# One decoder step on one core: the mixing and the routing of a block of tiles set in steps between the expert operations of the block before

## The reference, cut to what matters

```
g     = gelu(y);  y_s5 = rmsnorm(g * sigmoid(g @ w_glu), s5_norm_w)           # w_glu 1024 x 1024
y_m2  = group_rmsnorm(y_m2 * silu(z)) * m2_norm_w                             # two groups of 512
x     = x + concat([y_s5, y_m2]) @ w_out                                      # w_out 2048 x 1024
h     = rmsnorm(x, norm_ffn_w);   q = (h @ w_q) as 8 heads x 2 halves x 128   # w_q 1024 x 2048
s     = q . sub_keys (128 keys for each of the 16 halves)
sv,si = top_k(s, 16);  cand = sv[0][:, None] + sv[1][None, :];  cv, cpos = top_k(cand, 16)
idx   = si[0][cpos // 16] * 128 + si[1][cpos % 16];   gate = softmax(cv)      # 8 x 16 = 128 experts a row
x     = x + sum over the 128 experts: gate * gelu(u_tab[idx] . h) * v_tab[idx]
y     = rmsnorm(x, final_norm_w)
```

## Time and profile before

| | us |
|---|---|
| median of 3 runs (lowest to highest) | 4684.44 (4682.33 to 4685.42) |
| time of the profiled execution | 4684.25 |
| its span | 4682.5 |
| `mix_out` and the first routing, 1352.4 to 1891.6 | 539.20 |
| expert operations, 1891.6 to 4682.5 | 2790.90 |

### The profile page before, as it was taken

The page is one execution under the profiler, slowest core; times in us unless marked ns, Lnnn a source line. Parts: engine busy times, 40 slices in busy tenths (PEclk is TensorE's granted clock), DMA queues, the critical chain, the costliest instruction groups (busy, mean ns, idle before and its releaser), DMA issues.

```text
span 4682.5 us, 54327 instructions
## 1 busy us (share of the span) xinstructions
PE 2876.1 (61%) x17688; PEld 1481.5 (32%) x17688; DVE 2462.9 (53%) x4924; ACT 1290.2 (28%) x3117; POOL 1411.9 (30%) x1547
## 2 busy tenths in 40 slices
PE   8999590745559995554654744645645546447444
PEld 5766460723334444221311411411312213114110
DVE  1000529248831113576576675674675765766754
ACT  1110020112222321333333333333333333333332
POOL 3000320301100000444444444444443444444443
PEclk9999755866779997665755755756757658658555
DMA  4111300121131112899999999999999999999998
GB/s 163 52 50 36 75 2 2 43 101 30 39 160 66 46 54 97 349 421 420 415 421 400 421 421 405 420 420 404 420 419 400 421 419 405 421 407 420 421 415 362
DMA packets 258478, 1271.27 MB, mean 271 GB/s; under 512 B 63984, under 2 KB 98672, under 8 KB 118128
## 3 DMA queue, kind: packets, MB, share of 16 engines
q0 software_dynamic: 156672, 1140.92, 58.8%
q1 hardware_dynamic: 101536, 127.12, 8.2%
HBM read 1225.69 MB, written 40.09 MB: 270 GB/s over the span
## 4 chain that ended last, share of the span: by engine, by line
DMA 40%; issue 7%; PE 6%; ACT 4%; DVE 4%; POOL 1%; POOLq 0%; SPq 0%; DVEq 0%; ACTq 0%
DMA pe_ring<-in_uv,pe_index_now 39%; PE pe_acc L1858 3%; DVE pe_ring L1781 2%; PE pe_ps_q L1831 2%; ACT pe_mark L1629 1%; ACT pe_weight L1631 1%; PE pe_ps_t L1851 1%; ACT L1629 1%; DVE pe_work_a L1662 1%; POOL pe_ring L1570 1%; ACT L1620 1%; DMA pe_w_q<-in_w_q 0%; DVE pe_pos L1714 0%; DVE pe_work_b L1715 0%; PE pe_ps_s L1841 0%
## 5 line engine op out<-in xcount | busy, mean ns | idle before, releaser
L1781 DVE CUSTOM_DVE_ANT_0 pe_ring<-pe_ring,pe_h_rep 128x1024 f32<-128x1024 f32 x1088 | 1330.7, 1226 | 961.3 <-DMA pe_ring<-in_uv,pe_index_now 881.3
L1858 PE MATMUL pe_acc<-pe_ring,pe_weight 128*32 128x256 f32 x8704 | 1018.5, 560 | 1232.3 <-ACT pe_weight L1631 1203.4
L1570 POOL DMA_INDIRECT pe_ring<-in_uv,pe_index_now x1088 | 1198.0, 1101 | 1471.2 <-PE pe_acc L1858 1275.3
L1858 PEld LDWEIGHTS pe_acc<-pe_ring,pe_weight 128*32 128x32 f32 x8704 | 210.8, 131 | 1973.1 <-ACT pe_weight L1631 1863.6
L1629 ACT ACTIVATE pe_mark<-pe_eye,pe_dot 128x32 f32<-128x32 f32 x1088 | 349.4, 321 | 1744.1 <-DVE pe_dot L1781 1690.3
L1631 ACT ACTIVATE pe_weight<-pe_mark,pe_gate_now 128x32 f32<-128x32 f32 x1088 | 349.5, 321 | 35.1
L1831 PE MATMUL pe_ps_q<-pe_h_t,pe_w_q 128*128 128x128 f32 x2304 | 329.5, 303 | 1.9 <-DMA pe_w_q<-in_w_q 1.9
L1831 PEld LDWEIGHTS pe_ps_q<-pe_h_t,pe_w_q 128*128 128x128 f32 x2304 | 302.7, 213 | 60.1 <-issue 57.8
L372 PE MATMUL pj_bank<-pj_w_in,pj_normed_t 128*128 128x512 f32 (+1 forms) x720 | 267.6, 529 | 5.7 <-DMA pj_w_in<-in_w_in 5.7
L1392 PE MATMUL mo_ps_out<-mo_w_out,mo_both_t 128*128 128x512 f32 x576 | 251.1, 594 | 14.8 <-DVE mo_both_t L1342 11.9
L378 PE MATMUL pj_bank<-pj_normed_t,pj_w_in 128*128 128x128 f32 x1728 | 195.2, 275 | 0.0
...
## 6 DMA issues: line engine op xcount, KB each, us to landing
pe_ring<-in_uv,pe_index_now POOLq DMA_INDIRECT x1088
...
```

The source lines that it names most:

```text
L1570: nc.gpsimd.indirect_dma_start(out=ring[:, p, :], out_offset=None, in_=D["uv"], in_offset=bass.IndirectOffsetOnAxis(ap=row, axis=0)).then_ ...
L1781: V.tensor_tensor_reduce(out=ring[:, p, 0:D_MODEL], in0=ring[:, p, 0:D_MODEL], in1=h_rep[:, g % 2, :], scale=1.0, scalar=0.0, op0=ALU.mult ...
L1858: last = T.matmul(acc[j * PER:(j + 1) * PER, g % 2, 0:COLS], lhs(j), src[:, j * COLS:(j + 1) * COLS], start=first, stop=final)
```

## The change

`mix_out` becomes empty. `route_and_experts` now does mixing and routing for blocks of tiles: tile 0 alone, then tiles 1 and 2, tiles 3 to 5, tiles 6 to 8. Block 0 is done in an opening, with no expert operation beside it. Block 1 is set between the 128 operations of tile 0, block 2 between the 256 of tiles 1 and 2, block 3 between the 384 of tiles 3 to 5; tiles 6 to 8 have nothing between theirs. `block_steps` lists the steps of a block with a due time each, and `after[n]` holds the steps that follow operation n on every engine. 42% of the operations of a window (less 26) take the mixing, the others queries and keys. All loops are unrolled.

No weight matrix is held any more. `w_glu`, `w_out` and `w_q` are cut into 20 pieces of 256 columns ([128, 8, 256], 1.05 MB, rows of 1 KB in DRAM), loaded by SP into the two buffers of `w_buf`, once for every block. The load of a piece waits until the piece two before has been used. The gate matmuls have the weights as the stationary side and the block's tokens (128, 256 or 384) as the moving one, and so have the queries; the gate's result comes out transposed, and its norm is summed by a matmul with ones. The output matmuls move 256 columns of the weights for one tile's half. Chunk c of the gate matmuls waits for the sigmoid of chunk c - 2.

The ring has 7 slots instead of 8. `x_mid` stays in SBUF for the block, is stored to DRAM and read back as `x_now` tile by tile. Index and gate of a tile are double-buffered, so POOL copies no index. The keys of a block go through four units of four halves each, 16 steps a unit, each step for all tiles of the block. The places of the steps, in operations from the start of the window:

| | tile 0 (block 1) | tiles 1, 2 (block 2) | tiles 3 to 5 (block 3) |
|---|---|---|---|
| gate matmuls | 9 to 19 | 27 to 44 | 42 to 70 |
| output matmuls | 25 to 36 | 54 to 83 | 85 to 130 |
| h and its transposes | 39, 40 | 88 to 93 | 138 to 146 |
| queries and scores | 42 to 83 | 96 to 188 | 150 to 294 |
| keys | 54 to 101 | 122 to 227 | 191 to 354 |

```diff
@@ -1242,179 +1242,12 @@
 
 
 def mix_out(nc, D):
-
 def mix_out(nc, D):
...
+    pass
...
@@ -1423,482 +1256,693 @@
 
     PAIR = 2 * PH
     LEAST = -3.0e38
-    RING = 8
-    OPS = SLOTS
+    RING = 7
+    WB = 2
     GROUPS, PER = 4, 32
     COLS = D_MODEL // GROUPS
-    USES = OPS // RING
-    HALF = OPS // 2
-    UNITS, UNIT = PAIR // 4, 4
-    ROUTE_STEPS = 64
-    EVERY = OPS // ROUTE_STEPS
-    ROUTE_LINKS = UNITS * 4 + 27
-
-    SQUARES, NORM, TURN, H_T, QUERY = 3, 5, 6, 7, 8
-    Q_COPY, SCORE, SCORE_COPY, KEYS = QUERY + UNIT + 1, QUERY + UNIT + 2, QUERY + UNIT + 4, QUERY + UNIT + 5
-    SUMS = KEYS + UNIT * UNITS
-    EXP = SUMS + 16
-    CHOICE = SUMS + 22
-    assert CHOICE + 1 < (OPS - RING) // EVERY - 2
-    REP, REP_COPY, NOW_COPY = 16, 20, 14
-    assert GROUPS * PER == P and RING < HALF
+    BLOCK_OF = ((0,), (1, 2), (3, 4, 5), (6, 7, 8))
+    NB = max(len(tiles) for tiles in BLOCK_OF)
+    FIRST = [tiles[0] for tiles in BLOCK_OF]
+    HOME = {k: b for b, tiles in enumerate(BLOCK_OF) for k in tiles}
+    NT = MAIN_TILES * SLOTS + SAMPLE
+    NG = NT // PER
+    UNITS, UNIT = 4, 4
+    PIECES = 4 + 8 + PH
+    GLU, OUT, QUERY = 0, 4, 12
+    def block_steps(nb):
+        ev = []
+        add = lambda t, name, *args: ev.append((t, name, args))
+        for i in range(nb):
+            t = 8 * i
+            add(t, "sp_y", i)
+            add(t, "sp_x0", i)
+            for dt, name in ((2, "act_g"), (3, "dve_gate"), (3, "pe_g"), (4, "act_gt"), (4, "act_sq"), (5, "dve_mn"), (6, "pe_m"), (7, "dve_mt")):
+                add(t + dt, name, i)
+        g0 = 8 * (nb - 1) + 6
+        done = {}
+        for c in range(KT):
+            for dt, name in ((0, "pe_glu"), (1, "act_sig"), (2, "dve_s5"), (3, "act_ss"), (4, "pe_ss")):
+                add(g0 + 2 * c + dt, name, c)
+            done[GLU + c // 2] = g0 + 2 * c
+        r0 = g0 + 2 * KT + 3
+        add(r0, "act_r")
+        add(r0 + 1, "dve_r")
+        for c in range(KT):
+            add(r0 + 2 + c // 2, "dve_n", c)
+        o0 = r0 + 6 - nb
+        for q in range(4):
+            for half in range(2):
+                for i in range(nb):
+                    add(o0 + (2 * q + half) * nb + i, "pe_o", q, half, i)
+                done[OUT + 2 * q + half] = o0 + (2 * q + half) * nb + nb - 1
+            for i in range(nb):
+                add(o0 + (2 * q + 2) * nb + i, "dve_o", q, i)
+        h0 = o0 + 8 * nb + 1
+        for i in range(nb):
+            for dt, name in ((0, "act_hs"), (0, "sp_xm"), (1, "dve_h"), (2, "pe_h"), (3, "act_ht")):
+                add(h0 + 2 * i + dt, name, i)
+        q0 = h0 + 2 * nb + 2
+        for j in range(PAIR):
+            for dt, name in ((0, "pe_q"), (1, "act_q"), (2, "pe_s"), (3, "act_s")):
+                add(q0 + 3 * j + dt, name, j)
+            done[QUERY + j // 2] = q0 + 3 * j
+        for u in range(UNITS):
+            k0 = q0 + 12 * u + 13
+            for n in range(16):
+                add(k0 + n, "dve_k", u, n)
+            add(k0 + 12, "act_e", u)
+        for s in range(PIECES):
+            add(0 if s < WB else done[s - WB], "sp_w", s)
+        ev.sort(key=lambda e: e[0])
+        return ev, q0, ev[-1][0] + 1
+    opening = []
+    after = [[] for n in range(NT)]
+    for b, tiles in enumerate(BLOCK_OF):
+        ev, q0, last = block_steps(len(tiles))
+        if b == 0:
+            opening += [(name, (b,) + args) for t, name, args in ev]
+            continue
+        s, room = FIRST[b - 1] * SLOTS, len(BLOCK_OF[b - 1]) * SLOTS - 26
+        split = int(0.42 * room)
+        for t, name, args in ev:
+            n = s + (t * split // q0 if t < q0 else split + (t - q0) * (room - split) // (last - q0))
+            after[n].append((name, (b,) + args))
+    for k in range(TILES):
+        n = k * SLOTS
+        for back, name in ((31, "sp_x"), (20, "dve_hn"), (23, "pe_c"), (22, "dve_c")):
+            (after[n - back] if k else opening).append((name, (k,)))
+    for G in range(NG):
+        for back, name in ((16, "pe_rep"), (15, "act_rep")):
+            (after[G * PER - back] if G else opening).append((name, (G,)))
+        for on, name in ((0, "act_sum"), (1, "pe_add"), (3, "act_root"), (5, "dve_fin"), (6, "sp_st")):
+            after[min(G * PER + PER + on, NT - 1)].append((name, (G,)))
+    uses = [(name, args) for steps in [opening] + after for name, args in steps if name in ("pe_g", "pe_m", "pe_h", "pe_c", "pe_rep")]
+    TURN = {use: n for n, use in enumerate(uses)}
...
+            def weights(b, s):
+                W = PIECES * b + s
+                if W >= WB:
+                    b0, s0 = divmod(W - WB, PIECES)
+                    if s0 < OUT:
+                        sp.wait_ge(glu_made, KT * b0 + 2 * s0 + 2)
+                    elif s0 < QUERY:
+                        sp.wait_ge(out_made, outs(b0, (s0 - OUT) // 2, s0 % 2, size(b0) - 1))
+                    else:
+                        sp.wait_ge(q_made, PAIR * b0 + 2 * (s0 - QUERY) + 2)
+                if s < OUT:
+                    rows = D["w_glu"][:, :, s * COLS:(s + 1) * COLS]
+                elif s < QUERY:
+                    q, half = divmod(s - OUT, 2)
+                    rows = D["w_out"][:, KT - KT * half:2 * KT - KT * half, q * COLS:(q + 1) * COLS]
+                else:
+                    rows = D["w_q"][:, :, (s - QUERY) * COLS:(s - QUERY + 1) * COLS]
+                sp.dma_start(w_buf[:, W % WB], rows).then_inc(w_in[W % WB], 16)
+            def step(name, args):
+                if name == "sp_w":
+                    weights(*args)
...
+                if name == "act_sig":
+                    b, c = args
+                    C = KT * b + c
+                    act.wait_ge(glu_made, C + 1)
+                    if C >= 2:
+                        act.wait_ge(s5_made, C - 1)
+                    A(sig[:, c % 2, 0:width(b)], bg[:, c % 2, 0:width(b)], ACT.Sigmoid).then_inc(sig_ready, 1)
...
+            def keys(b, u, n):
...
+                if n == 0:
+                    dve.wait_ge(s_ready, UNITS * (U + 1))
+                    settle(dve, settled)
+                    for j, i in each:
+                        last = V.max(out=best[:, j, i, 0:8], in_=score[:, j, i, :])
+                    chain.link(last)
+                    settle(dve, settled)
...
+                if name == "dve_c":
+                    k = args[0]
+                    u = TURN["pe_c", args]
+                    dve.wait_ge(turned, u + 1)
+                    V.transpose(choice[:, k % 2], ps_t[:, 0:2, :]).then_inc(taken, 1)
+                    dve.wait_ge(taken, u + 1)
+                    V.tensor_copy(index[:, k % 2, :], choice[:, k % 2, 0, :]).then_inc(index_ready, 1)
...
+                if name == "pe_glu":
+                    b, c = args
+                    W, C = PIECES * b + GLU + c // 2, KT * b + c
+                    if c == 0:
+                        pe.wait_ge(taken, TURN["pe_g", (b, size(b) - 1)] + 1)
+                    if c % 2 == 0:
+                        pe.wait_ge(w_in[W % WB], 16 * (W // WB + 1))
+                    if c >= 2:
+                        pe.wait_ge(sig_ready, C - 1)
+                    for kk in range(KT):
+                        last = T.matmul(bg[:, c % 2, 0:width(b)], w_buf[:, W % WB, kk, c % 2 * P:(c % 2 + 1) * P], wide(in_t_all, b)[:, kk, :],
+                                        start=kk == 0, stop=kk == KT - 1)
+                    last.then_inc(glu_made, 1)
...
+                if name == "pe_o":
+                    b, q, half, i = args
+                    W = PIECES * b + OUT + 2 * q + half
+                    if i == 0:
+                        pe.wait_ge(w_in[W % WB], 16 * (W // WB + 1))
+                    if (q, half, i) == (0, 0, 0):
+                        pe.wait_ge(taken, TURN["pe_m", (b, size(b) - 1)] + 1)
+                        pe.wait_ge(sig_ready, KT * b + KT)
+                    if half == 0 and q * size(b) + i == 2:
+                        pe.wait_ge(r_root, b + 1)
+                    if (q, half, i) == (0, 1, 0):
+                        pe.wait_ge(s5_ready, KT * b + KT)
+                    if q * size(b) + i >= 4 and half == 0:
+                        pe.wait_ge(out_taken, kept(b, q, i) - 4)
+                    src = wide(s5_t_all if half else m2_t_all, b)
+                    for kk in range(KT):
+                        last = T.matmul(bg[:, (q * size(b) + i) % 4, 0:COLS], src[:, kk, i * P:(i + 1) * P], w_buf[:, W % WB, kk, :],
+                                        start=half == 0 and kk == 0, stop=half == 1 and kk == KT - 1)
+                    last.then_inc(out_made, 1)
...
+            for n in range(NT):
+                k, G, p = n // SLOTS, n // PER, n % RING
+                if n % SLOTS == 0:
+                    pe.wait_ge(x_now_in, 16 * k + 16)
+                if n % PER == 0:
+                    if G >= 2:
+                        pe.wait_ge(y_ready, G - 1)
```

(5 more changed lines are left out.)

946 lines of the change are left out of this document (435 added, 511 removed).

## The result

The change is slower, by 0.4%: 4701.53 us (median of 6 runs, 4696.99 to 4707.38) against 4684.22 for the kernel before in the same session, ratio 1.0038 (95% interval 1.0025 to 1.0051). The forecast was 4655 and faster. 4701.53 lies inside the forecast's wide range, but on the other side of the kernel before. The profiled execution has a span of 4695.2, 42 more than the 4653 of the sum.

The account below looks back on a forecast made before the run. The prediction took the expert stage to be bound by DMA bytes. First gather at 1528, plus 2980 of bytes, plus 145 of stalls made a span of 4653 us, time 4655, range 4565 to 4772.

Parts of the forecast that it names:

- Stalls: 54 + 45 + 15 + 20 + 10, about 145: Expert stage: keys 54, gate 45, output 15, loads and chain of h 20, tile boundaries 10; 60 to 240 us.
- 364 saved: Start of the stage: first expert gather at about 1528 instead of 1891.6, 364 us saved.
- 18 us of keys: Tiles 1 and 2: three tiles' keys on DVE take 301 us against 283, 18 lost; tiles 3 to 5 none.
- the gate "near nothing": Gate phase after tile 0: PE and ACT overlap, 6.6 us of PE against 6.5 of DMA, near nothing lost at full clock.
- the output "covered": Output phase after tile 0: matmuls covered at full clock; the 15 us term came from tile 0's 64 against 51.
- shares of 45, 20 and 10: Stall terms: gate phase over three windows 45 us, loads and chain of h 20, tile boundaries 10.
- The late pieces: Rival, 36 mixing pieces: with two buffers and 23 us a piece PE waits, 104 us instead of 60; 4700, 5%.
- some 10 us of cover: Gather ring: seven slots last 17.4 us, of which some 10 cover waits, as operations hold their slots.
- Nothing of these 232 us is hidden: Expert stage: 180 us of weight pieces and 52 of tile loads and stores add fully, as DMA is already full.
- PE's clock: Rival, mixing in the three windows: at clock 0.6, 187 us over DMA's where the forecast has 60; 4782, 25%.
- The stalls were not hidden: Rival, expert stage: the ring covers the stalls, leaving bytes plus some 40 us as before; 4548, 17%.
- No change to speak of: Rival, whole kernel: the same sum with 165 to 185 us of stalls; 10%.

Follow-up runs that it names:

- e4: The change with only the first of the two picks of a key unit computed, so other experts are gathered; 4660.19 us, 0.9934 against the kernel before.
- e18: The change with its ring at a multiple of 512 and its weights in rows of 8 KB; 4638.92 us, 0.9900 against the kernel before.
- e2: The change with blocks 1 to 3 loading only an eighth of each weight piece's bytes; 4611.87 us, 0.9836 against the kernel before.
- e7: The change with the gate's sigmoid computed by tanh, the ring staying at its address; 4686.40 us, 1.0005 against the kernel before.

## Why the prediction was wrong

**The step that failed** is the last term of the sum, "Stalls: 54 + 45 + 15 + 20 + 10, about 145": net of the 43 that the kernel before had, 102 us were to be added to the bytes, and 144 were. The sum was a balance of 364 saved against nearly as much spent, 29 us apart, so 42 more turned it. The kernel before shows where they are (us from the windows above; weights, x and y by q1's share of the DMA engines):

| | tile 0 | tiles 1, 2 | tiles 3 to 5 | rest |
|---|---|---|---|---|
| longer than before | 146 | 140 | 88 | 1 |
| of it q1's packets | 79 | 83 | 69 | 0 |
| what is left | 67 | 57 | 19 | 1 |

The bytes came to 231, for 232. In tile 0 the prediction had most of its stalls. For tiles 1 to 5 it had 18 us of keys, the gate "near nothing" and the output "covered" at full clock, and shares of 45, 20 and 10 that it does not split; there 76 are left. These causes were found:

- **The keys in tiles 1 and 2.** One pick of two is worth 21 us there (e4), where the prediction had 18 for all keys.
- **The late pieces.** The arithmetic was right, 23 us for a piece beside gathers against the 25.5 of the chain, and I put it at 5% with 4700 and at nothing in the sum. I said that it costs nothing as long as the engines move bytes; but PE stands still with the ring full behind it, and then no gather is issued. Two buffers and 1 KB rows make PE wait: long rows alone take 30 us off the change, a third buffer 17 off the windows of the kernel with six slots. Of the long rows' gain a part is bytes; in tiles 3 to 5 e18 gives 14 of 20 to shorter packets and leaves 6 for the lateness.
- **The lost slot.** The sum counts with some 10 us of cover from seven slots; how much less that is than with eight, and in how many places, I didn't work out. In the blocks of two the eighth slot is worth 18.5 us; going from seven to six cost 45 in the change itself, nearly all in tiles 1 to 5. It could not be tried with blocks of three, for want of memory.
- **The pace.** The gathers' 2.486 us belongs to an address. In the change the ring lies at 480 above a multiple of 512, before at 192; the median from dot to dot in the last tiles is 2.492 and 2.484. That is at most 1088 x 0.008, 9 us of the 42, and less where the gathers don't set the time. The change was not meant to move it.

The sizes are measured, most of them in a neighbouring kernel. That they add up to the 42 is not shown: a slot more also covers a late piece, so they overlap.

**What was luck.** That the term missed by no more than 42 is due to a second error. The sum adds stalls to bytes. By e2 tile 0's window gets back 7 of 52 us of bytes and that of tiles 1 and 2 21, so some 75 us of bytes were hidden there, and the engines' own stalls in these windows are larger than what is left in the table by about that (an estimate from e2's windows).

**What held.** The opening: 175.2 for 176. The bytes: q1's shares of the four windows, 16.5%, 11.2%, 7.3% and 0.9%, are 254 us, for 257 forecast with what the stage carried. The gate's turn and the keys on DVE: e7 and e4 confirm both as stalls. Operations 54 to 101 took 178.1 us, for 173. Tiles 6 to 8 run at full DMA.

**What did not, beside the sum.** "Nothing of these 232 us is hidden" is wrong for tile 0: without seven eighths of its weights the window is 7 us shorter, not 52. There DMA idles 11% and the weights fill gaps. In the same window a cost was larger than its term: with the Gelu, Silu and roots of its two tiles the first ten dots take 1535 to 1575, 40 us, partly as the second tile's y is loaded only when the first is used up (a wait of 10.2 us for it stands in the chain).

**The rivals.** PE's clock did not decide: it was 0.89 to 0.95 in the output phases and the later gate phases, far above the 0.71 at which that rival begins. The stalls were not hidden. "No change to speak of", with 165 to 185 of stalls, comes nearest in the sum: taken as the sum takes them they were 186, and the kernel is still a little past it. The late pieces came true, though not alone.

**The rule of the Trainium skill** on turns between queues ("DMA: Bandwidth & Descriptors", Queues, rings and completion order) was the one that spoke against this change. The 25.4 to 26.3 us for a piece in tile 3's chain agree with it (the 13.9 and 16.9 of tiles 1 and 2 are shorter), and I should have let it weigh more. The section states the turns; that they speak against weights beside a gather is my reading of it.
